# Two product parts of an attention step stand around the transposes of the probabilities, ahead of the outputs

## What is computed

```python
qc, kc, vc, glu_c = project(h_ctx)      # h @ w_in, split in q, k, v, u, gate
ql, kl, vl, glu_l = project(h_lat)
# per grid row of 64 tokens and per head, over 8x16 neighbours and the 256 context tokens
s_loc = einsum('bchd,bacwhd->bhcaw', q_r, k_win) + bias
s_ctx = einsum('bchd,bnhd->bhcn', q_r, k_ctx)
p = softmax(concatenate([s_loc, s_ctx], axis=-1), axis=-1)
o = einsum('bhcaw,bacwhd->bchd', p_loc, v_win) + einsum('bhcn,bnhd->bchd', p_ctx, v_ctx)
out_lat = concatenate([att_lat, conv_module(glu_l)], axis=-1) @ w_out
```

## Time and profile before

| | us |
|---|---|
| median of 3 runs | 1931.53 |
| lowest and highest | 1930.30, 1933.77 |
| the profiled execution | 1933.99 |
| its span in the trace | 1932.2 |

### The profile page before, as it was taken

The page is one execution under the profiler, slowest core; times in us unless marked ns, Lnnn a source line. Parts: engine busy times, 40 slices in busy tenths (PEclk is TensorE's granted clock), DMA queues, the critical chain, the costliest instruction groups (busy, mean ns, idle before and its releaser), DMA issues.

```text
span 1932.2 us, 26676 instructions
## 1 busy us (share of the span) xinstructions
PE 1771.3 (92%) x10600; PEld 1465.6 (76%) x10600; DVE 834.7 (43%) x1265; ACT 559.8 (29%) x901; POOL 67.7 (4%) x104
## 2 busy tenths in 40 slices
PE   5999999898999999999999569898889899999997
PEld 4888876687888888888887457666657677887886
DVE  4687776335222222222224334655644443333333
ACT  3344444524211112211222213333233332122221
POOL 0321101000000000000000000000000000000000
PEclk8999999999999999999999568988859999999999
DMA  7613332121224322251235000010003322332233
GB/s 307 95 49 121 127 127 76 66 65 44 65 65 148 125 64 65 98 185 55 65 124 199 29 11 33 22 44 22 23 12 123 105 69 94 93 92 90 95 98 109
DMA packets 47315, 169.01 MB, mean 87 GB/s; under 512 B 5392, under 2 KB 5648, under 8 KB 47120
## 3 DMA queue, kind: packets, MB, share of 16 engines
q1 hardware_dynamic: 31408, 115.47, 18.8%
q10 hardware_dynamic: 15072, 51.53, 7.3%
q0 software_dynamic: 768, 1.08, 0.8%
HBM read 163.83 MB, written 4.19 MB: 87 GB/s over the span
## 4 chain that ended last, share of the span: by engine, by line
PE 86%; DVE 7%; ACT 2%; DMA 2%; issue 1%; SPq 0%; ACTq 0%; DVEq 0%
PE PS L425 58%; PE PS L1644 8%; PE PS L1538 3%; PE PS L1547 2%; PE PS L1687 2%; PE PS L1779 2%; PE PS L1881 2%; PE PS L1880 1%; DMA scr<-in_ada 1%; PE PS L1703 1%; DVE scr L1417 1%; PE PS L1855 1%; PE PS L1554 1%; PE PS L1669 1%; PE PS L1599 1%
## 5 line engine op out<-in xcount | busy, mean ns | idle before, releaser
L425 PE MATMUL PS<-h_hi,w_hi 128*128 128x512 f32 (+1 forms) x1296 | 399.7, 363 | 3.7 <-DVE w_lo L410 3.2
L425 PE MATMUL PS<-h_lo,w_hi 128*128 128x512 f32 (+1 forms) x1296 | 393.8, 358 | 0.0
L425 PE MATMUL PS<-h_hi,w_lo 128*128 128x512 f32 (+1 forms) x1296 | 393.6, 358 | 0.0
L410 DVE TENSOR_TENSOR w_lo<-raw,w_hi 128x1024 fp32r<-128x1024 f32 x196 | 239.6, 1224 | 259.4 <-ACT w_hi L405 247.1
L405 ACT ACTIVATE w_hi<-raw 128x1024 fp32r<-128x1024 f32 x196 | 206.2, 1052 | 284.5 <-PE PS L425 241.6
L425 PEld LDWEIGHTS PS<-h_hi,w_hi 128*128 128x128 f32 x1296 | 217.3, 192 | 48.1 <-DVE w_lo L410 5.6
L425 PEld LDWEIGHTS PS<-h_lo,w_hi 128*128 128x128 f32 x1296 | 216.3, 191 | 36.5
L425 PEld LDWEIGHTS PS<-h_hi,w_lo 128*128 128x128 f32 x1296 | 215.6, 191 | 37.0
L425 PE MATMUL PS<-c_hi,w_hi 128*128 128x512 f32 (+1 forms) x688 | 215.8, 367 | 24.8 <-DVE c_lo L1018 18.7
L425 PE MATMUL PS<-c_hi,w_lo 128*128 128x512 f32 (+1 forms) x688 | 211.9, 361 | 0.0
L425 PE MATMUL PS<-c_lo,w_hi 128*128 128x512 f32 (+1 forms) x688 | 211.6, 361 | 0.0
(11 more groups left out here) (255 smaller groups left out, 1820.5 us busy)
## 6 DMA issues: line engine op xcount, KB each, us to landing
raw<-in_w SPq DMA_DIRECT2D x196, 512.0 KB, 3.5
scr<-in_ada ACTq DMA_DIRECT2D x48, 512.0 KB, 5.5
adaw<-in_ada ACTq DMA_DIRECT2D x32, 512.0 KB, 4.5
scr<-in_ada SPq DMA_DIRECT2D x8, 1024.0 KB, 10.3
X<-in_xT SPq DMA_DIRECT2D x4, 768.0 KB, 6.7
X<-in_xT ACTq DMA_DIRECT2D x1, 3072.0 KB, 10.1
x_spill<-X ACTq DMA_DIRECT2D x1, 2048.0 KB, 9.3
X<-x_spill ACTq DMA_DIRECT2D x1, 2048.0 KB, 8.8
```

Source lines behind the costliest of these rows:

```text
L410: nc.vector.tensor_tensor(w_lo[:, j], raw[:, j].rearrange("p (k n) -> p k n", k=KT), w_hi[:, j].bitcast(f32), ALU.subtract).then_inc(s_lo, 1)
L425: last = nc.tensor.matmul(G[j][:, a:b], w[:, j, k], m[:, k, a:b], start=(n == 1), stop=(n == 3 * k_tiles))
```

## The change

In each step `transpose_probs(U)` moves from directly behind the scores to behind the part of slot 2U, and the part of slot 2U+1 moves from the end of the step to directly behind the transposes, ahead of `attend(U)`. No instruction is added or taken away, and the code of the other engines is the same.

```diff
                 if U + 1 < NU:
                     scores(U + 1)
-                transpose_probs(U)
                 a, b, a1, b2 = finished(U)
...
                 part = slot_part(2 * U)
                 if part:
                     ab_product(*part)
+                transpose_probs(U)
+                part = slot_part(2 * U + 1)
+                if part:
+                    ab_product(*part)
                 attend(U)
...
                         ada_row(adaw[:, a % 2], 3, 2 + a % 2)
-                part = slot_part(2 * U + 1)
-                if part:
-                    ab_product(*part)
```

## The result

The changed kernel takes 1989.1 us, the median of four runs (1985.2 to 1994.3), against 1931.1 for the kernel before; the ratio is 1.030 with a 95% interval of 1.0272 to 1.0327. It is slower, by 58 us in the medians; on another chip of the study it was slower by 52 (ratio 1.0273, 1.0255 to 1.0290). The profiled execution took 1987.15 us with a span of 1985.4, so 53.2 us more than the span before.

What follows compares the result with a forecast made beforehand. PE was taken as the bound, busy 1771.3 of 1932.2 us; waits of 21.5 + 7.4 + 3.4 + 7.3 - 0.7 = 38.9 plus 12 for the clock made 51, so 1931.5 + 51 = 1983 us, range 1962 to 2000.

Steps and rivals of the forecast that it cites:

- Evictions behind the first part: Steps 1, 4, 7, 10, 13: PE stands from the transposes' end until the finished product is evicted; 21.5 us.
- Evictions behind the second part: Steps 3, 6, 9, 12: PE waits for the eviction of a product that ended in the second part; 7.4 us.
- Column sums and V: In seven steps, column sums of q and k and V's transposes wait for ACT's modulation-row copy; 3.4 us.
- Steps 15 to 18: PE waits for convolution taps, for ACT's copy ahead of the outputs and for modulation values; 7.3 us in all.
- The gain in step 9: PE's wait ahead of the transposes of step 9 would go away; -0.7 us.
- The clock: Seven waits of 3 us or longer are each followed by half-speed work, 1.7 us each; 12 us in all.
- the clock that stays up: Rival: PE's clock does not fall, as PE works hard between waits 10 us or more apart; 1970 us, chance 0.12.
- the waits that feed each other: Rival: DVE becomes the bound in most steps, 13 others each losing 1 to 2 us; 1997 to 2009, chance 0.10.
- cover in part: Rival: ACT reaches evictions earlier than its order says, halving their term; 1965 or less, down to 1950, chance 0.09.
- the gain: Rival: idle weight loads of transposes and outputs are hidden, some 11 us with step 9's wait; 1920 us, chance 0.03.
- One sign of being wrong: The prediction is wrong if the time ahead of 137 us or behind the attention moves.

Runs made afterwards that it cites:

- the run that evicts first: Changed kernel, with ACT evicting the product of the first part before copying the transposed probabilities in steps 1, 4, 7, 10, 13; ratio 1.0091, median 1956.5 us.
- the run with five steps: Kernel before, with the new order only in steps 1, 4, 7, 10 and 13; ratio 1.0171, median 1965.2 us.
- the filler run: Changed kernel, with matmuls nobody reads put in five waits, run beside the changed kernel on one chip; ratio 1.0214, median 1975.1 us.
- the run with all covered again: Changed kernel, with ACT/DVE evictions earlier, two more taps ahead of `normalise`, and transposes behind the scores from step 15 on; ratio 1.0009.
- the second half alone: Kernel before, with only the second part moved ahead of the outputs and the transposes left directly behind the scores; ratio 1.0035.
- the first filler run: Changed kernel, with matmuls nobody reads put in the five waits between transposes and second part, first measurement; ratio 1.0202.

## Why the prediction was right, and where its terms were off

I had put 1983 us with 1962 to 2000; the median is 1989.1. In the attention the trace shows 50.9 us more, where the terms sum to 51. So close a sum is partly luck: the waits were put at 38.9 and PE stood 36.0 longer, the clock at 12 and PE was busy 14.9 longer. Term by term, by the trace:

- *Evictions behind the first part:* 21.5 us put, 3.80 + 4.06 + 3.80 + 4.36 + 5.27 = 21.3 measured, from rows of the kernel before in which the same chain ran under cover. Shown by the run that evicts first and by the one with five steps. This was the step on which the sign rested.
- *Evictions behind the second part:* 7.4 put; 1.90 + 2.92 + 1.21 + 0.97 = 7.0 measured.
- *Column sums and V:* 3.4 put. On the matmuls the list shows 0.7, but their weight loads waited 2.8 and 0.7 us for L767, 3.5 in all: the wait is there, at the engine's loads. The 2.8 us between the two figures do not count as standing in PE's rows.
- *Steps 15 to 18:* 7.3 put. The taps came 4.06 us late (3.8 put). Ahead of the outputs from step 15 on PE waits 12.1 us against 9.4. Step 16's transposes wait 0.75 for the modulation values (1.3 put), and step 17's no longer wait 1.17: 4.06 + 2.7 + 0.75 - 1.17 = 6.3.
- *The gain in step 9:* 0.7 put, none measured. This step failed. I took that wait for one for the probabilities. The timeline of the kernel after shows what it is, in step 9 and in step 16 alike: DVE's `mod_add` (L989), and PE's transposes 0.1 us behind its end.

```profile
273.54 0.15 DVE L989 TENSOR_TENSOR mod<-PS,small 128x4 f32<-128x4 f32 x1
...
273.80 1.58 PE L1687 MATMUL PS<-c_early,scr 128*128 128x128 f32 x9 [0.66 <-issue]
```

```profile
376.76 0.15 DVE L989 TENSOR_TENSOR mod<-PS,small 128x4 f32<-128x4 f32 x1
...
377.02 1.13 PE L1687 MATMUL PS<-c_early,scr 128*128 128x128 f32 x8 [0.75 <-issue]
```

  The transposes wait for the modulation values of the step before, which stand last but one in DVE's step. PE comes one part later in the new order, but DVE does too, since its exponentials come later; the wait stays. In the list it is put down to "issue", which names no releaser. The trace of the kernel before has the same pair in step 9:

```profile
242.96 0.16 DVE L989 TENSOR_TENSOR mod<-PS,small 128x4 f32<-128x4 f32 x1
...
243.21 2.50 PE L1687 MATMUL PS<-c_early,scr 128*128 128x128 f32 x16 [0.67 <-issue]
```

- *The clock:* 12 put as 7 x 1.7. All seven falls are in the trace: five of 6.8 us behind the evictions, and one of 3.4 each behind u3 and behind the taps. The five cost about 2.4 us each by the filler run, not 1.7, and the one behind u3 1.5: the term of a single fall was sized too low. I had shrunk the 2.65 of the earlier trace rows in proportion to the wait; but the fall begins while PE still waits, and the part behind it runs its 5.7 us almost wholly at half speed. The term as a whole lies between two readings. PE's busy time gives 14.9. With the weight loads' waits counted as waits, 50.9 - 21.3 - 7.0 - 3.5 - 6.3 - 0.5 (two small ones in steps 0 and 1) = 12.3 are left. That 12 comes so near is not a proof of its working: behind the same five waits the run with five steps had three falls of half the length.

The half-speed time of the attention grew by 41 us. The Trainium skill, TensorE: Matmul & The Clock Gate, section Terms, would charge half of it, 20.5; the trace leaves 12.3 to 14.9. I had argued that only the time in which PE works should be charged. That explains a part: PE was busy for 35.2 of the 41 us, and half of these is 17.6, still above what the trace leaves. Where the rest goes is open.

Of the rivals, the clock that stays up is refuted by the windows of step 1, the waits that feed each other by the run with five steps, cover in part by the five waits, and the gain by the weight loads' gaps: those at the outputs are 4.7 us (4.6 before), and those at the transposes fell from 6.0 to 1.8. In the run with all covered again they are 4.6 and 0.9, and the output projection still comes 5.0 us late.

One sign of being wrong was a move of the time behind the attention. It moved by 2.3 us, which lies within the spread of that rest over the runs.

The rest of the difference to the medians, 58.0 against the 53.2 of the profiled spans, is the spread of the runs, 1985 to 1994 after and 1930 to 1934 before.

## What to carry to other kernels

Before moving a piece of work on one engine, list for each buffer that it frees or fills what the *other* engine has queued ahead of the release: a product that is finished in PSUM is not free until the evicting engine has passed everything ahead of it in its own order. Read the price of an uncovered chain from the old trace, where it ran under cover; for the five evictions here it came out to 1%. And lay the orders of all engines together: the same edit of ACT was worth 30 us with one order of PE and cost 18 us with the other.

## What the runs showed of the hardware

- Each of the waits of 3.8 to 5.3 us cost more than itself. The clock was at 1.2 GHz when PE restarted, and the next part took 5.7 us instead of 3.4. Matmuls of no use in the wait (28 in step 1) kept 2.4 GHz, and five such fillers made the kernel 12.7 us faster: 0.6% gained by added work.
- With the transposes moved alone, no wait of PE was above 2.2 us, yet the granted clock fell seven times in the attention; the second half alone, with five waits of 1.0 to 1.9, had one fall, 1.2 us behind the last of them. What in the first of these runs brought the clock down was not isolated.
- The length of a wait does not decide it alone. The prediction took some 2 us as the mark; the same wait of 2.9 us for u3 was followed by half speed in both traces of the changed kernel and in the first filler run, and by none in the second.
